# A one-core, two-block transformer kernel: filler matmuls at two layer norms taken out, and four pieces of vector work put elsewhere in their queues

## The reference, cut to what matters

```python
# first block, layer 1: an S5 state-space mixer
u, z = split(x @ a_w_in, 2)                       # 1024 + 1024 columns
bbar = complex factors(lam, dt) * b               # per group and state
h_t = a * h_{t-1} + bbar * u_t                    # complex scan over the 256 tokens
y = Re(c * h) + d_skip * u
g = gelu(y)
y = g * sigmoid(g @ w_glu + b_glu)
x = layer_norm(alpha * x + (y * silu(z)) @ w_out)
# first block, layer 2: shared key/value matmul, compressed/selected/window attention with gates
x = layer_norm(alpha * x + (gated attention) @ b_w_out)
# second block
proj = rmsnorm(x) @ w_in                          # q, k, v of 8 differential and 8 stick-breaking heads
diff = rmsnorm(softmax(q1 k1) v - lam * softmax(q2 k2) v)
z = q @ k.T * scale                               # stick-breaking head
a = exp(log_sigmoid(z) + reverse_cumsum(strict * log_sigmoid(-z)))
sb = rmsnorm(a @ v)                               # per head
x = x + concat(diff, sb) @ w_out
x = x + relu(rmsnorm(x) @ w_mlp_in)**2 @ w_mlp_out
out = rmsnorm(x)
```

## Time and profile before

| | |
|---|---|
| median of three runs | 2070.38 us (2067.76, 2070.38, 2070.98) |
| profiled execution, its own time | 2067.76 us |
| its span in the profile | 2066.0 us |
| PE busy / weight loads | 2033.2 us (98%) / 1791.4 us |
| DVE, ACT, POOL busy | 1292.5, 971.5, 71.3 us |
| granted TensorE clock, mean | 0.999 |
| DMA | 360.87 MB, 175 GB/s on average |

### The profile page before, as it was taken

The page is one execution under the profiler, slowest core; times in us unless marked ns, Lnnn a source line. Parts: engine busy times, 40 slices in busy tenths (PEclk is TensorE's granted clock), DMA queues, the critical chain, the costliest instruction groups (busy, mean ns, idle before and its releaser), DMA issues.

```text
span 2066.0 us, 32038 instructions
## 1 busy us (share of the span) xinstructions
PE 2033.2 (98%) x12561; PEld 1791.4 (87%) x12561; DVE 1292.5 (63%) x1770; ACT 971.5 (47%) x1408; POOL 71.3 (3%) x84
## 2 busy tenths in 40 slices
PE   8999999999999999999999999999999999999998
PEld 7898898888989898889899898888888888888886
DVE  6798755456666666658666666556546555655655
ACT  5554544344444444446445546544434434434443
POOL 2000021000000000100000001000000000000000
PEclk9999999999999999999999999999999999999999
DMA  8345576545455554755454544566666666666663
GB/s 284 93 138 196 165 219 209 171 133 173 141 160 149 154 162 134 243 171 170 161 167 153 160 153 151 199 184 189 195 189 191 192 193 186 187 198 186 189 197 103
DMA packets 202935, 360.87 MB, mean 175 GB/s; under 512 B 25360, under 2 KB 33904, under 8 KB 202160
## 3 DMA queue, kind: packets, MB, share of 16 engines
q1 hardware_dynamic: 200656, 351.88, 55.2%
q0 software_dynamic: 1664, 5.97, 0.9%
q10 hardware_dynamic: 480, 1.10, 0.1%
HBM read 356.03 MB, written 2.10 MB: 173 GB/s over the span
## 4 chain that ended last, share of the span: by engine, by line
PE 89%; DVE 6%; issue 2%; ACT 2%; DMA 0%; ACTq 0%; POOL 0%; DVEq 0%; POOLq 0%
PE acc L515 35%; PE acc L519 19%; PE banks L515 8%; PE banks L1099 6%; PE acc L1099 6%; PE banks L1102 3%; PE acc L1102 3%; DVE w_low L1737 1%; PE acc L605 1%; PE banks L868 1%; ACT w_high L1143 1%; PE acc L546 1%; PE banks L896 1%; PE banks L807 1%; PE banks L985 1%
## 5 line engine op out<-in xcount | busy, mean ns | idle before, releaser
L1737 DVE TENSOR_TENSOR w_low<-raw,w_high 128x1024 fp32r<-128x1024 f32 x648 | 791.9, 1229 | 620.6 <-ACT w_high L1143 618.8
L1143 ACT ACTIVATE w_high<-raw 128x1024 fp32r<-128x1024 f32 x648 | 682.7, 1059 | 741.3 <-PE acc L515 326.4
L519 PE MATMUL acc<-x_high_low,w_high 128*128 128x256 f32 x2432 | 357.1, 285 | 0.7 <-issue 0.7
L515 PE MATMUL acc<-w_high,x_high_low 128*128 128x512 f32 x1152 | 328.6, 398 | 0.0
L519 PEld LDWEIGHTS acc<-x_high_low,w_high 128*128 128x128 f32 x2432 | 318.5, 192 | 3.5 <-issue 2.2
L515 PEld LDWEIGHTS acc<-w_high,x_high_low 128*128 128x128 f32 x1152 | 214.1, 188 | 43.5 <-issue 0.5
L519 PE MATMUL acc<-x_high_low,w_low 128*128 128x256 f32 x1216 | 195.3, 283 | 0.0
L515 PE MATMUL acc<-w_low,x_high_low 128*128 128x512 f32 x576 | 178.4, 391 | 0.0
L515 PE MATMUL acc<-w_high,h_high 128*128 128x512 f32 x544 | 169.1, 392 | 3.0 <-DVE w_low L1737 1.1
L515 PE MATMUL acc<-w_low,h_high 128*128 128x512 f32 x544 | 167.7, 389 | 0.0
L515 PE MATMUL acc<-w_high,h_low 128*128 128x512 f32 x544 | 167.5, 389 | 0.0
(11 more groups left out here) (379 smaller groups left out, 2169.4 us busy)
## 6 DMA issues: line engine op xcount, KB each, us to landing
raw<-in_b_w_in SPq DMA_DIRECT2D x128, 512.0 KB, 3.8
raw<-in_w_mlp_in SPq DMA_DIRECT2D x128, 512.0 KB, 3.7
raw<-in_w_mlp_out SPq DMA_DIRECT2D x128, 512.0 KB, 4.5
raw<-in_w_in SPq DMA_DIRECT2D x96, 512.0 KB, 3.7
raw<-in_kv_w SPq DMA_DIRECT2D x48, 512.0 KB, 3.8
raw<-in_a_w_in SPq DMA_DIRECT2D x32, 512.0 KB, 5.8
raw<-in_b_w_out SPq DMA_DIRECT2D x32, 512.0 KB, 4.5
raw<-in_w_out SPq DMA_DIRECT2D x32, 512.0 KB, 4.6
```

The source lines that it names most:

```text
L515: ins_ = nc.tensor.matmul(PAIRS[pair][:, t, :], xa[:, kt + j, t * P:(t + 1) * P], wa[:, k, j, :], start=first and n == 0, stop=last and n ...
L519: ins_ = nc.tensor.matmul(ACC[pair][:, m // 2, (m % 2) * TOK:(m % 2 + 1) * TOK], wa[:, k, j, m * P:(m + 1) * P], xa[:, kt + j, :], start=f ...
L1143: nc.scalar.activation(WH[:, s % SPLIT, :, :], RAW[:, s, :, :], ACT.Copy).then_inc(hi_ready, SLOTS + 1 if first_one else 1)
L1737: V.tensor_tensor(WL[:, k, :, :], RAW[:, p % SLOTS, :, :], WH[:, k, :, :].bitcast(F32), ALU.subtract).then_inc(lo_ready, SLOTS + 1 if isin ...
```

## The change

It makes five edits. (1) `keep_busy` and its four calls go. (2) In the state-space stage DVE does `b_powers` of the next quarter one tick later and behind `inputs`, and ACT does `b_spread` one tick later. (3) Four small instructions (the GLU bias and two rounded constants) move from tick 13 to tick 12 on DVE. (4) The four multiplies by 0.25 z move behind the gate multiplies, one after each. (5) For the second four stick-breaking heads, the mean square moves from i = 4h + 8 to 4h + 9, the root on POOL from 4h + 8 to 4h + 10, and `normed` to 4h + 10 for every head; before it stood at 4h + 8 for heads 0 and 1 (inside the block of head h + 2, between its min/abs and its wait for the logarithm) and at 4h + 9 for heads 2 and 3. What is computed stays the same.

```diff
@@ -561,13 +561,6 @@
                 ins_ = nc.tensor.transpose(BK[b][:, kt % 4 * P:(kt % 4 + 1) * P], X[:, t, kt * P:(kt + 1) * P], ID)
             ins_.then_inc(tr_full, 2 if n == 4 else 1)
 
-        def keep_busy(group, n):
-
-            pe.wait_ge(acc_free, group - 1)
-            for i in range(n):
-                nc.tensor.matmul(ACC[group % 2][:, i % 2, :], ID_R[:, :], HH[:, 2 * i:2 * i + 2, :].rearrange("p k t -> p (k t)"),
-                                 start=True, stop=True)
-
         def split_ready(first):
             return lambda s: pe.wait_ge(split_done, first + s + 1)
 
@@ -779,10 +772,7 @@
         pe.wait_ge(acc_free, G_AOUT + 2)
         tiles_apart(U_AOUT + 1, (G_AOUT + 3) % 2, CB, True, HH, HL)
         for n in range(6):
-            if n == 4:
-                keep_busy(G_KV, 7)
             tile_turn(TR_X1, n)
-        keep_busy(G_KV, 4)
 
         def later_turns(s):
             if s in (1, 3):
@@ -924,10 +914,7 @@
             tick((U_BOUT + 3) * SLOTS + s, s, "rows", (G_BOUT + 3) % 2, 2 * s, s == 0, False, HH, HL)
         tiles_apart(U_BOUT + 3, (G_BOUT + 3) % 2, 2 * SPLIT, False, HH, HL)
         for n in range(6):
-            if n == 4:
-                keep_busy(G_QKV, 7)
             tile_turn(TR_H, n, 8)
-        keep_busy(G_QKV, 4)
 
 
         def root_columns():
@@ -1346,7 +1333,7 @@
             if tau == 11:
                 taps_copy(0)
                 diagonals(1)
-            if tau == 13:
+            if tau == 14:
                 b_spread(1)
             if tau == 15:
                 b_copy(1)
@@ -1361,7 +1348,7 @@
             if tau == 18:
                 taps_copy(1)
                 diagonals(2)
-            if tau == 19:
+            if tau == 20:
                 b_spread(2)
             if tau == 21:
                 b_copy(2)
@@ -1375,7 +1362,7 @@
             if tau == 24:
                 taps_copy(2)
                 diagonals(3)
-            if tau == 25:
+            if tau == 26:
                 b_spread(3)
             if tau == 27:
                 b_copy(3)
@@ -2024,10 +2011,10 @@
                     rotations(q, 0)
                     rotations(q, 1)
                 if tau == first:
-                    if q < 3:
-                        b_powers(q + 1, 0)
-                        b_powers(q + 1, 1)
                     inputs(q)
+                if tau == first + 1 and q < 3:
+                    b_powers(q + 1, 0)
+                    b_powers(q + 1, 1)
                 if tau == first + 2 or (q == 3 and tau == first + 1):
                     states(q)
                 if tau == first + 3:
@@ -2037,7 +2024,7 @@
             if tau == 6:
                 steps.inc(V.memset(MHALF[:, :], -0.5))
                 steps.inc(V.memset(TINY[:, :], 0.0))
-            if tau == 13:
+            if tau == 12:
                 v.wait_ge(params_done, 2)
                 V.tensor_scalar(PT[:, 0, 72:80], PT[:, 0, 72:80], 0.5, None, ALU.mult, ALU.bypass).then_inc(glu_bias, 1)
                 v.wait_ge(const_rest, 16)
@@ -2056,21 +2043,19 @@
         low(0)
         y_split(3)
         low(0, 3)
-        for k in range(0, 8, 2):
-            g_, z_ = flat(YT[:, k:k + 2, :]), flat(ZT[:, k:k + 2, :])
-            steps.inc(V.scalar_tensor_tensor(g_, g_, 0.25, z_, ALU.mult, ALU.mult))
-        steps.wait()
         for c in range(2):
             for b in range(2):
                 part()
                 part()
                 g_ = flat(YT[:, 4 * c + 2 * b:4 * c + 2 * b + 2, :])
+                z_ = flat(ZT[:, 4 * c + 2 * b:4 * c + 2 * b + 2, :])
                 ins_ = V.scalar_tensor_tensor(g_, ACC[c][:, b, :], 1.0, g_, ALU.add, ALU.mult)
                 if b:
                     ins_.then_inc(acc_free, 1)
                     v.wait_ge(acc_free, G_GLU + c + 1)
                 else:
                     steps.link(ins_)
+                steps.link(V.scalar_tensor_tensor(g_, g_, 0.25, z_, ALU.mult, ALU.mult))
                 kt = CB + 4 * c + 2 * b
                 if c:
                     low(0)
@@ -2500,16 +2485,12 @@
                     if i == 4 * h + 7:
                         head_split(order, 4 * j + h)
                 else:
-                    if j and i == 4 * h + 8:
-                        mean_square(order)
                     if i == 4 * h:
                         v.wait_ge(sb_full, n + 1)
                         s_ = BK[0][:, 0:384]
                         a, b, c = SA[:, r, :], SB[:, r, :], SC[:, r, :]
                         steps.link(V.tensor_scalar(b, s_, 0.0, None, ALU.min, ALU.bypass))
                         V.scalar_tensor_tensor(a, b, 2.0, s_, ALU.mult, ALU.subtract).then_inc(sb_abs, 1)
-                        if j and h >= 2:
-                            normed(order - 2)
                         v.wait_ge(sb_act, 3 * n + 2)
                         steps.link(V.tensor_tensor(b, b, a, ALU.subtract))
                         steps.link(V.tensor_tensor(c, b, s_, ALU.subtract))
@@ -2519,9 +2500,9 @@
                         v.wait_ge(sb_summed, n + 1)
                         b = SB[:, r, :]
                         V.tensor_tensor(b, b, BK[1][:, 0:384], ALU.add).then_inc(f_dve, 1)
-                    if j == 0 and i == 4 * h + 7:
+                    if i == 4 * h + (9 if j else 7):
                         mean_square(order)
-                    if i == 4 * h + (9 if j else 8) and not (j and h < 2):
+                    if i == 4 * h + (10 if j else 8):
                         normed(order)
                     if i == 4 * h + (13 if j else 10):
                         head_split(order, 8 + 4 * j + h)
@@ -2763,13 +2744,11 @@
                     if i == 4 * h + 4:
                         head_rsqrt(order)
                 else:
-                    if j and i == 4 * h + 8:
-                        head_rsqrt(order)
                     if i == 4 * h + 5:
                         pool.wait_ge(sb_act, 3 * n + 3)
                         d = SA[:, n % 2, :].rearrange("p (b q) -> p b q", b=3)[:, 0:3:2, :]
                         GP.tensor_tensor(d, d, const("strict").unsqueeze(1).to_broadcast([P, 2, P]), ALU.mult).then_inc(f_pool, 1)
-                    if j == 0 and i == 4 * h + 7:
+                    if i == 4 * h + (10 if j else 7):
                         head_rsqrt(order)
 
         for j in range(2):
```

## The result

The changed kernel takes 2084.39 us (median of 4; 2082.32 to 2089.77) against 2070.48 us (4; 2067.76 to 2070.98): ratio 1.0074, 95% interval [1.0051, 1.0097]. Slower, as forecast, but by 13.9 us between the medians where I had 8.4. The four times are 2082.32, 2082.59, 2086.20 and 2089.77 us, so the median stands between two pairs that are 3.6 us apart or more. The profiled execution took 2082.4 us, span 2080.6: 14.6 us more than the profiled one of before.

The account below looks back on a forecast made before the run. TensorE, busy 2033.2 of 2066.0 us, bounds the kernel, so new waits are paid. Edits 2, 3, 4, 5 and 1 give 0.9 + 0 + 2.8 + 4.65 + 0 = 8.4 us on the 2070.4 median: 2078.8 us, range 2076 to 2081 (8 in 10: 2074 to 2085).

Parts of the forecast that it names:

- wait after tick 15: State-space stage, quarter 1: TensorE's transposes newly wait 3.3 us for the later `b_powers` and ACT's spread.
- tap wait: Tap blocks of quarter 1: TensorE's existing 2.48 us wait until 98.67 would absorb most of the 3.3 us lateness.
- z wait: First GLU tick: TensorE already waits 1.62 us for DVE at 162.57; GLU was to start 0.9 us late.
- 3.3 late against that wait leaves TensorE 0.2 late: Tap blocks of quarter 1: lateness of 3.3 us set against the 2.48 us wait leaves 0.2 us.
- by the same order: Quarter 2, state-space stage: `b_powers` ends at 107.7, the spread at 109.9, leaving TensorE 0.95 us late.
- wait ahead of `b_turn`: Quarter 2 transposes in the state-space stage: a new TensorE wait of 0.75 us, repeated in quarter 3.
- POOL's root fits under the `low`: W_OUT, head 0: POOL's root takes 0.69 us, hidden under a VectorE `low` of 1.14 us.
- I take 0 for the sum: Both layer norms: removing the fillers gains nothing, and a possible clock loss there was left open and counted as 0.
- Rival A: Clock falls at both norms, 2.6 to 5 us, possibly at the new gaps too; 2083, up to 2088 us; chance 0.36.
- B: W_OUT: DVE finishes head 2's block early enough that edit 5 costs nothing; 2074.2 us; chance 0.09.
- C: Both norms: the fillers slow DVE and ACT through shared memory, so removal speeds the kernel; 2072 us; chance 0.03.
- D: GLU waits: edit 2 absorbed and edit 4 partly; 2077 us, counted inside the main forecast's chance of 0.52.

Follow-up runs that it names:

- e5: e2 plus twelve unread filler matmuls on TensorE ahead of `b_turn(1)`: 2070.15 us.
- e11: Edits 2 to 5 with `keep_busy` as before, plus the fillers of e5 and e6: 2079.72 us, ratio 1.005.
- e3: The kernel before with edit 4 alone (the four multiplies behind the gate multiplies): 2073.23 us, ratio 1.0014.
- e6: e4 plus 24 unread filler matmuls ahead of the turns of each of heads 0 and 1 in W_OUT: 2077.20 us, ratio 1.0032.
- e1: The kernel before with edit 1 alone (no filler matmuls at the two layer norms): 2074.05 us, ratio 1.0019.
- e2: The kernel before with edits 2 and 3 alone: 2072.16 us, ratio 1.0013.
- e4: The kernel before with edit 5 alone: 2077.55 us, ratio 1.0041.
- e12: The changed kernel run again, nothing altered: 2082.10, 2082.20, 2082.25, 2087.22 and 2089.13 us.
- e7: As e4, but `normed` and POOL's root at i = 4h + 9, directly behind the mean square: 2075.35 us, ratio 1.0025.
- e8: The kernel before with ten unread filler matmuls in TensorE's wait ahead of the taps of quarter 1: 2068.64 us, median ratio 0.9993.

## Why the prediction was wrong in size

Sign, places and the kind of cost were right; the sum was 3.5 us short for the lower group of the changed kernel even after an error in the base that went the other way. From the lower group of before, 2067.8, to the lower group of the changed kernel, 2082.3, are 14.5 us. My 8.4 are short of that by 6.1 (the median of the result, 2084.39, is 2.1 above that group again, for the clock at the norms):

| term | forecast | measured (from) |
|---|---|---|
| edit 2, waits | 0.9 | 2.3 (e5, e11) |
| edit 4 | 2.8 | 2.9 (e3, changed, e11) |
| edit 5, waits | 4.65 | 6.25 (e6, e11) |
| edit 1, fillers in the way | 0 | 0 (e1) |
| clock after tick 15 | 0 | 1.1 (e2 less e5) |
| clock in W_OUT, first fall | 0 | 1.6 to 1.7 (e4 less e6, changed less e11) |
| clock at the norms | 0 | 3.8 (e1) or 4.7 (e12), by their times in 4 of 10 executions |

The rows without the norms come to 14.2 us, which is the ledger's 14.21. The 0.3 us left of the 14.5 are the later start of the changed kernel's profiled execution (0.39).

*Edit 2.* The wait after tick 15 is there (2.98 us, forecast 3.3), and the tap wait has fallen to 0.39. In e5, without the fall of the clock, TensorE is late by 0.92, 2.02 and 3.13 us at the taps of quarters 1 to 3, where I had 0.2, 0.95 and 1.7; the shorter z wait (1.62 to 0.79) gives back the 0.8 that I had. Two steps failed. The first is "3.3 late against that wait leaves TensorE 0.2 late". By its own numbers it leaves 0.8 (3.3 less 2.48), and the 0.2 comes near only with a second wait just ahead, which I didn't name:

```profile
95.09 1.10 PE L694 MATMUL banks<-u_cols,skip_diagonals 128*128 128x256 f32 x4 [0.53 <-ACT y_cols L1298]
```

In e5 TensorE is 3.6 us late behind the transposes (2.98, 0.18 for the second wait within them, the rest around the interruptions). It gets back these 0.53 and 2.09 of the tap wait; 0.39 us of that wait stays, as in every quarter: it is ACT's copy of what TensorE has only just made. The second step is that "by the same order" VectorE has `b_powers` of quarter 2 done at 107.7. Between `inputs` and `b_powers` there now stands a `low` that waits for ACT's `high`; the row is from e5, which started 1.08 us late:

```profile
104.21 1.23 DVE L1740 TENSOR_TENSOR w_low<-raw,w_high 128x1024 fp32r<-128x1024 f32 x1 [0.73 <-ACT w_high L1146]
```

With these 1.08 us taken off, `b_powers` ends at 108.4, and TensorE starts these transposes 1.6 us late instead of 0.95. I also priced the wait ahead of `b_turn` (0.53 us, forecast 0.75) and nothing within it: ACT comes to its copies straight from the late spread and a `high`, and TensorE waits once more between the transposes (0.18 us at 113.34). From the taps of one quarter to those of the next this makes 1.1 us in all, where I had 0.75. This split is read from one profile and was not tried by itself.

*Edit 4.* Right. No cover was left, and each of the four multiplies is paid.

*Edit 5.* The two waits are at their places, but 2.97 and 2.86 us instead of 2.55 and 2.1. The step that failed is "POOL's root fits under the `low`". It starts 0.17 us after a `low` has started, ends 0.55 after that `low`, and takes 1.60 us; VectorE then waits for it. With no `low` beside it, in e7, it takes 0.69. My duration came from a place without a `low` in progress. The two waits make 5.8 of the 6.25 us; the other 0.4 I did not trace. The Trainium skill ("SBUF — State Buffer", section "SBUF: two separate sides") has GpSimd and a VectorE operation with two inputs in that memory take turns for the whole instruction on a port pair that they share; the row agrees.

*Edit 1 and the clock.* "I take 0 for the sum" failed. Rival A named the mechanism and the size (2.6 to 5 us for both norms, measured 3.8 and 4.7) and said that the new gaps could do it too. I argued against it from one row, 94.50 to 98.60, in which the clock stayed up through a wait of 2.48 us. That was one execution: in e3, e4, e6 and e7 the clock falls behind this very wait, which costs 1.0 to 2.4 us. (Eight transposes in a low stretch take 1.93 us in e12, at 245.58. That bears out the reading of the earlier trace rows, though the profile has the clock at 1.00 there.) The two waits that the change adds, 2.98 and 2.97 us, had the clock fall behind them in every profile of edits 2 and 5 (or behind the second, in e4) unless fillers stood there or the wait was 2.06 us and less (e7).

*The base.* I added to the median, 2070.4, and held the 2.6 us to the profiled 2067.76 for chance. e8 shows that it is not chance: with fillers in the tap wait the median falls by 2.2 us. Edit 2 takes that wait away, so these 2.2 to 2.6 us had to come off again. This error hid part of the others.

*Other rivals.* B (cover in W_OUT) fell: the block ended when I said. C (fillers in the way) fell by e1. D (edit 2 absorbed, edit 4 partly) fell: edit 2 costs 2.3 us of waits and edit 4 the full 2.9.

What stays open: why the norms lose the clock in e1's profile and in four executions of the changed kernel (one by its profile, three by their times) and not in its other six, while e1 by its times lost it there in nearly all. The stretches there are alike, and no run varied the length of the wait by itself. Nor do the times settle each single execution: one of the six, 2082.32 us, has a mean clock of 0.996 where the others have 0.998, so a fall somewhere may have cost it nearly nothing.

## What to carry to other kernels

- Before adding to a median, look whether its executions lie in groups. If they do, find the group of the profiled execution, and ask whether the change touches the place that makes the groups.
- Price a wait of 2.5 to 3 us of TensorE as the wait and a likely fall of the clock (1 to 2.4 us here); one execution in which the clock held says little. A filler matmul is cheap where it hides, and what it guards isn't seen in the row where it stands.
- A wait can pay for lateness only down to what the engine waits for its own results (0.39 of 2.48 us here). And take a duration from a row with the same neighbours: POOL's root cost 0.69 or 1.60 us by what VectorE did beside it.

## Unexpected of the hardware

- The granted clock falls to 0.50 behind a wait of 2.5 us that another execution of the same instructions passes at 1.00: for at least 6.4 us in e3 (0.70 and 0.50 over 4 us each), not at all in the profile of before. Behind the wait of 2.98 us of the changed kernel it fell for 3.4 us (0.79 over the 8 us from 77). Over all executions of before it makes two groups of times, 2067.6 to 2068.5 and 2070.1 to 2071.6 us.
- A POOL operation on 128x2 values at 1.60 instead of 0.69 us when a VectorE operation with two inputs is in progress as it starts; started before one (1298.74, `low` from 1298.95) it took 0.69.
